# Two passes over one weight block: the value weights of a second transformer block streamed twice

## The chip, the cores and the metric

The kernel runs on one core of one Trainium2 chip. It computes two transformer blocks for 256 tokens and 16 meta tokens in float32. The metric is the device time of one execution in microseconds; lower is better.

## The reference, cut to what matters

```python
def reference(...):
    x = first_block(...)        # hybrid mixer, then peer_ffn: 8 heads x 16 experts of 16384 for each token
    return second_block(x, ...)

# second_block, for h = [meta tokens; x], 272 tokens of 1024
a = rmsnorm_2(h, norm_mix_g[i])
proj = a @ w_in[i]
q, k, v, qi, ki, wi, cu, cb, cc, ga, gb = jnp.split(proj, PROJ_SPLITS, axis=-1)
y_attn = dsa_attention(q, k, v, qi, ki, wi) @ w_attn_out[i]
y_conv = (cb * short_conv(cc * cu, conv_w[i])) @ w_conv_out[i]
mixed = jax.nn.sigmoid(ga) * y_attn + jax.nn.sigmoid(gb) * y_conv
h = h + mixed @ w_out[i]
```

The values `v` are a product of all 272 tokens with a 1024 by 1024 part of `w_in`. A token's values need only that token's row of `a`.

## The kernel before, in words

**The weight stream.** Every weight matrix is cut into blocks of 128 x 1024 float32 (512 KB), which lie in DRAM in the order of their use (`stages`, `FIRST`, `COUNT`). SyncE (SP) loads them one after another into `ring`, which has four slots. ScalarE writes the rounded high part of a block to `w_hi` (`split_hi`), VectorE the rest to `w_lo` (`split_lo`), and TensorE multiplies in three products: high by high, high by low, low by high. Both splits run two blocks ahead of use (`ahead`, LEAD = 2). Three waits tie this together: SP loads block b when block b - 4 has its low part (L398), `split_hi` of block b waits until TensorE has begun enough blocks that block b - 4 is done with (`block_begun`, L327), and TensorE waits for the low part (`parts_ready`).

**Feature and value blocks.** `column_block` makes a tile of 128 features by all tokens: 24 matmuls of 272 columns (L505). `value_blocks` makes tiles with the tokens on the partitions. It takes the blocks in pairs, and for each pair there are three token tiles (meta tokens, tile 0, tile 1), each of 24 matmuls of 256 columns (L540, L543, L546). ScalarE and VectorE evict the tiles in turn (L1011, L1468). The second block's `w_in` runs as 44 feature blocks, 8 value blocks, 16 gate blocks, the last of these with the attention of 16 head-tiles beside them.

**The gathers.** Before that comes the expert layer of the first block. For each of two tiles of 128 tokens there are 128 slots, so 256 (`SLOTS`). For each slot GpSimd issues an indirect DMA that brings a row of 8 KB for each token into one of eight buffers (`gathered`, L457). VectorE takes the dot product of the row's first half with the token (`dot`, L1792). ScalarE makes from it a coefficient and a diagonal matrix (`coefficient`, L1200, L1203, L1207, four `diag` buffers), and TensorE adds the row's second half, scaled by the diagonal, to a sum in PSUM (`add_row`, L803: two float32 matmuls, which show as four records). Its semaphore `row_used` lets GpSimd issue the gather eight slots on. VectorE also chooses the experts of later slots meanwhile (`route_step`), up to slot 223; ScalarE changes its function table twice in every sixteenth slot of these.

The second tile's slots are used for more. Tile 0's sums are finished after slot 127, and in slots 131 to 160 they are normed, transposed and split into the operand of the second block (`x_hi`, `x_lo`), and so are the meta tokens (`early_hi`, `early_lo`, L1253, L1852). Tile 1 follows only after slot 255 (L1815 to L1852), and then the second block's feature blocks begin.

Each engine runs its instructions in the order written; every wait is on a semaphore.

Of the kernel before, what the change touches and what calls it, by code (L numbers as in the profile page):

```python
# [107 lines left out]
BANK = [g % 2 if g < TILE0["w_out"] else g % BANKS for g in range(TILES)]  # L108
ORD = [BANK[:g].count(BANK[g]) for g in range(TILES)]
BEFORE = [[BANK[:g].count(bank) for bank in range(BANKS)] for g in range(TILES + 1)]  # L110
# [9 lines left out]
def build(nc, stream, rows_dram, small_dram, keys_dram, kiwi_dram, gain_dram, x_dram, gain_rows_dram, meta_2_dram, out_dram):  # L120
    with ExitStack() as ctx:
# [8 lines left out]
        work = sb("work", [P, NKEYS * REAL])  # L130
# [14 lines left out]
        meta_tok = sb("meta_tok", [META, D])  # L145

# [17 lines left out]
        def carve(sizes, offsets=None):  # L164

            at, parts = 0, {}
            for name, n in sizes:
                parts[name] = work[:, at:at + n]
                if offsets is not None:
                    offsets[name] = at  # L170
                at += n
            assert at <= NKEYS * REAL, at
# [7 lines left out]
                     ("gx", 2 * T), ("gl", 2 * T), ("nbc", 4), ("dq", 2 * REAL), ("eqm", 2 * REAL), ("eqw", 2 * P),  # L180
                     ("km", 2 * META), ("kx", 2 * P),
                     ("ke", KEY_BUFS * P), ("kt", KEY_BUFS * P), ("A", 4 * W), ("A0", 4 * REAL), ("qall", 10 * REAL),
                     ("mix", C * REAL), ("sil", 4 * REAL), ("keys", KEYS_COLS), ("sq", C * T)],
                    one_at)
        feat = one["feat"].rearrange("p (n t) -> p n t", n=16)
# [44 lines left out]
        assert base <= one_at["sq"], base  # L230
# [6 lines left out]
        two = carve([("feat2", 60 * T), ("v2", 3 * D), ("kidup", T), ("wi", 16), ("score", 2 * T),  # L237
# [5 lines left out]
        v2 = two["v2"].rearrange("p (k n) -> p k n", k=3)  # L243
# [16 lines left out]
        sq_late = work[:, NKEYS * REAL - C * T:]  # L260
# [10 lines left out]
        tile_taken = [sem(f"tile_taken{i}") for i in range(BANKS)]  # L271
# [95 lines left out]
        def tiles_are_taken(eng, g):  # L367

            for bank in range(BANKS):
# [109 lines left out]
        def _(pe):  # L479
# [43 lines left out]
            def value_blocks(name, between=None):  # L523
# [4 lines left out]
                xh, xl = x_parts[T]  # L528
                for n in range(COUNT[name] // 2):
                    b, g = FIRST[name] + 2 * n, TILE0[name] + 3 * n  # L530
                    k = b % RING
                    parts_ready(b + 1)
                    for j in range(3):
                        bank_is_free(pe, g + j)
                        out = bank_of(g + j)[:, 0:2 * COLS].rearrange("p (k n) -> p k n", k=2)
                        at = META + (j - 1) * P if j else 0
                        for c in range(C):
                            hi = w_hi[:, k:k + 2, c * P:(c + 1) * P]
                            lo = w_lo[:, k:k + 2, c * P:(c + 1) * P]
                            i = mm(out, xh[:, c, at:at + P], hi, start=c == 0, stop=False)  # L540
                            if c == j == 0:
                                i.then_inc(block_begun, 1)
                            i = mm(out, xh[:, c, at:at + P], lo, start=False, stop=False)  # L543
                            if c == j == 0 and n:
                                i.then_inc(block_begun, 1)
                            last = mm(out, xl[:, c, at:at + P], hi, start=False, stop=c == C - 1)  # L546
                        last.then_inc(tile_ready, 1)
                        if between is not None:
                            between(3 * n + j)

# [167 lines left out]
            value_blocks("w_in_values", lambda n: mixing(n + 4))  # L718
# [117 lines left out]
            for n in range(SLOTS):  # L836
# [8 lines left out]
                elif n == SLOTS // 2 + 26:  # L845
                    turn_meta()

# [28 lines left out]
            for n in range(4):  # L876
                column_block(b0 + n, g0 + n, T, operand=X_MIX if n == 0 else None)
# [30 lines left out]
            value_blocks("w_in_2_values")  # L908
# [1205 lines left out]
```

## Time and profile before

| | |
|---|---|
| median of 3 runs | 1428.22 us (1428.22 to 1432.86) |
| profiled execution | 1428.08 us, span 1426.3 us |
| PE busy, weight loads busy | 1237.0 us (87%), 864.4 us (61%) |
| VectorE, ScalarE, GpSimd busy | 865.6 (61%), 638.7 (45%), 264.5 us (19%) |
| moved by DMA | 378.27 MB, of these 268.45 by the row gathers |
| mean granted TensorE clock | 0.978 of full |

The span runs from the first to the last instruction. A busy PE is an average over stages of different kinds, so the stages have to be read one by one. Idle time of an engine that doesn't set the pace costs nothing.

### The profile page before, as it was taken

To read this page: it belongs to the slowest core of one execution; us is meant where nothing else is said; L and a number is where in the kernel's file an instruction comes from. 1 tells how busy PE (TensorE), PEld (TensorE's weight loads), DVE (VectorE), ACT (ScalarE), POOL (GpSimd) and SP (SyncE) were. 2 spreads that over 40 slices of the span, in tenths; PEclk is the share of its full clock that TensorE was granted. 3 is DMA by queue.
4 is the path that set the end of the run, shared out by engine and by line. 5 is a ranking of instruction groups with operands and counts; after the bars stand their busy time and mean duration, and the time that the engine had idled before them with its cause. 6 is when DMAs were issued, how large, how long until landed. Compare 5 with 4: busy or idle time off the path is not lost.

```text
span 1426.3 us, 19005 instructions
## 1 busy us (share of the span) xinstructions
PE 1237.0 (87%) x6408; PEld 864.4 (61%) x6408; DVE 865.6 (61%) x1839; ACT 638.7 (45%) x1422; POOL 264.5 (19%) x300
## 2 busy tenths in 40 slices
PE   6999887787777778787778777999999989999998
PEld 4888774232222223332222224999999989899976
DVE  6743568666666667776666545567735546644454
ACT  5654443444443444544443434344435563443344
POOL 4000004333333333343333330000000020000000
PEclk9999999999999999999999999999999999999999
DMA  6321338999999999999999993345533345455543
GB/s 216 134 89 61 106 121 350 421 422 420 422 420 422 421 422 421 381 423 422 421 421 422 421 422 147 115 156 172 177 123 130 105 147 165 146 184 185 183 165 108
DMA packets 67351, 378.27 MB, mean 265 GB/s; under 512 B 7488, under 2 KB 7616, under 8 KB 34384
## 3 DMA queue, kind: packets, MB, share of 16 engines
q0 software_dynamic: 36864, 268.45, 45.4%
q1 hardware_dynamic: 30128, 107.85, 23.0%
q10 hardware_dynamic: 288, 1.08, 0.2%
q8 instruction: 37, 0.61, 0.2%
q14 instruction: 34, 0.28, 0.1%
HBM read 376.30 MB, written 1.05 MB: 265 GB/s over the span
## 4 chain that ended last, share of the span: by engine, by line
PE 50%; DMA 33%; DVE 7%; ACT 5%; issue 4%; DVEq 0%; SPq 0%; ACTq 0%
DMA work<-in_rows,work 32%; PE ps L505 28%; PE ps L803 6%; PE ps L866 4%; DVE w_lo L336 2%; PE ps L540 2%; PE ps L543 1%; PE ps L546 1%; ACT work L1207 1%; DVE work L1792 1%; ACT w_hi L328 1%; ACT work L1203 1%; DVE work L1951 1%; PE ps L942 1%; PE ps L733 1%
## 5 line engine op out<-in xcount | busy, mean ns | idle before, releaser
L803 PE MATMUL ps<-work 128*128 128x512 f32 x1024 | 508.6, 628 | 138.1 <-ACT work L1207 137.9
L803 PEld LDWEIGHTS ps<-work 128*128 128x128 f32 x1024 | 181.4, 194 | 461.7 <-ACT work L1207 313.6
L1792 DVE CUSTOM_DVE_ANT_0 work<-work,ps 128x1024 f32<-128x1024 f32 x256 | 312.4, 1220 | 219.9 <-DMA work<-in_rows,work 219.7
L457 POOL DMA_INDIRECT work<-in_rows,work x256 | 240.3, 939 | 600.2 <-PE ps L803 389.0
L336 DVE TENSOR_TENSOR w_lo<-ring,w_hi 128x1024 fp32r<-128x1024 f32 x198 | 242.5, 1229 | 151.5 <-ACT w_hi L328 150.1
L505 PE MATMUL ps<-x_hi,w_hi 128*128 128x256 f32 (+1 forms) x1248 | 315.6, 293 | 11.7 <-ACT x_hi L346 6.3
L505 PE MATMUL ps<-x_lo,w_hi 128*128 128x256 f32 (+1 forms) x1248 | 307.3, 287 | 0.0
L505 PEld LDWEIGHTS ps<-x_hi,w_hi 128*128 128x128 f32 x1248 | 236.5, 193 | 18.6 <-issue 10.1
L505 PEld LDWEIGHTS ps<-x_lo,w_hi 128*128 128x128 f32 x1248 | 236.0, 192 | 0.3
L328 ACT ACTIVATE w_hi<-ring 128x1024 fp32r<-128x1024 f32 x198 | 205.5, 1052 | 57.3 <-PE ps L866 28.1
L1200 ACT ACTIVATE work<-work 128x1 f32<-128x1 f32 x256 | 51.9, 203 | 350.8 <-DVE work L1792 349.3
L505 PE MATMUL ps<-x_hi,w_lo 128*128 128x256 f32 (+1 forms) x1248 | 179.6, 287 | 0.0
L505 PEld LDWEIGHTS ps<-x_hi,w_lo 128*128 128x128 f32 x1248 | 164.9, 192 | 0.0
L1011 ACT ACTIVATE work<-ps 128x272 f32<-128x272 f32 (+2 forms) x96 | 37.6, 392 | 188.6 <-PE ps L505 146.4
L1207 ACT ACTIVATE work<-ident,work 128x128 f32<-128x128 f32 x256 | 102.7, 401 | 8.4
L1203 ACT ACTIVATE work<-work 128x1 f32<-128x1 f32 x256 | 75.4, 294 | 8.3
L471 POOL TENSOR_TENSOR work<-work 128x256 f32<-128x256 f32 x8 | 8.6, 1102 | 284.9 <-ACT work L1367 280.8
L540 PE MATMUL ps<-w_hi,x_hi 128*128 128x256 f32 x192 | 55.4, 289 | 0.0
L546 PE MATMUL ps<-w_hi,x_lo 128*128 128x256 f32 x192 | 54.0, 281 | 0.0
L543 PE MATMUL ps<-w_lo,x_hi 128*128 128x256 f32 x192 | 53.9, 281 | 0.0
L1394 ACT ACTIVATE work<-ps 128x256 f32<-128x256 f32 x22 | 8.4, 383 | 65.4 <-PE ps L505 65.4
L540 PEld LDWEIGHTS ps<-w_hi,x_hi 128*128 128x128 f32 x192 | 36.1, 188 | 1.9 <-issue 1.3
(278 smaller groups left out, 1068.5 us busy)
## 6 DMA issues: line engine op xcount, KB each, us to landing
ring<-in_stream SPq DMA_DIRECT2D x198, 512.0 KB, 3.3
work<-in_rows,work POOLq DMA_INDIRECT x256, 15.3
res<-in_tokens SPq DMA_DIRECT2D x4, 272.0 KB, 3.8
gain_rows<-in_gain_rows SPq DMA_DIRECT2D x1, 1024.0 KB, 9.4
out_dram<-work SPq DMA_DIRECT2D x4, 256.0 KB, 2.3
work<-in_kiwi ACTq DMA_DIRECT2D x1, 544.0 KB, 3.5
work<-in_keys SPq DMA_DIRECT2D x1, 512.0 KB, 8.1
work<-in_gain ACTq DMA_DIRECT2D x1, 512.0 KB, 3.3
```

What stands on the lines that cost most here:

```text
L328: nc.scalar.activation(w_hi[:, k, :], ring[:, k, :], ACT.Copy).then_inc(w_hi_ready, 1)
L336: nc.vector.tensor_tensor(w_lo[:, k, :], ring[:, k, :], w_hi[:, k, :].bitcast(F32), ALU.subtract).then_inc(w_lo_ready, 1)
L457: g.indirect_dma_start(out=gathered[:, n % ROWS, :], out_offset=None, in_=rows_dram, in_offset=bass.IndirectOffsetOnAxis(ap=expert[:, n:n ...
L505: last = mm(out, w[:, k, c * P:(c + 1) * P], x[:, c, skip:], start=n == 0, stop=n == 3 * C - 1)
L540: i = mm(out, xh[:, c, at:at + P], hi, start=c == 0, stop=False)
L543: i = mm(out, xh[:, c, at:at + P], lo, start=False, stop=False)
L546: last = mm(out, xl[:, c, at:at + P], hi, start=False, stop=c == C - 1)
L803: last = mm(ps[:, Y_BANK[t] + j, :], diag[:, n % DIAGS, :], gathered[:, n % ROWS, D + 512 * j:D + 512 * j + 512], start=False, stop=k == S ...
L866: last = mm(ps[:, 4 + 2 * t + j, :], x[:, at:at + P], w[:, k, 512 * j:512 * j + 512], start=False, stop=True, skip_group_check=True)
L1203: link(a(route["coef"][:, n:n + 1], route["gelu"][:, n:n + 1], ACT.Copy, scale=route["gate"][:, n:n + 1]))
L1207: a(diag[:, n % DIAGS, :], ident[:, :], ACT.Copy, scale=route["coef"][:, n:n + 1]).then_inc(diag_ready, 1)
L1792: v.tensor_tensor_reduce(R["product"][:, D * (n % 2):D * (n % 2) + D], gathered[:, n % ROWS, 0:D], ps[:, bank:bank + 2, :].rearrange("p b ...
```

## The change: what it does

The 8 value blocks of the second block stand twice in the stream. The first copy (`w_in_2_values_0`) stands ahead of the feature blocks. Its two tiles of each pair, meta tokens and tile 0, are made during the gathers, one tile every 10 slots from slot 170 to slot 240, into PSUM banks 4 and 5; ScalarE splits a block three slots after each tile and evicts the tile five slots after it, VectorE splits its low part four slots after. The second copy stands in the old place, and there only tile 1 is made. The number of blocks grows from 198 to 206. The values of the meta tokens go to `meta_tok`, those of tile 0 to a buffer of their own; `work` shrinks to make room, and some of its scratch parts move. The first feature block now signals for the last early block too (`owed`).

```diff
@@ stages, TILE0 and banks @@
-              ("w_in_2_features", 44),
+              ("w_in_2_values_0", 8), ("w_in_2_features", 44),
...
-                  ("w_in_2_features", 44), ("w_in_2_values", 12),
+                  ("w_in_2_values_0", 8), ("w_in_2_features", 44), ("w_in_2_values", 4),
...
+WORK = 30080
+PSUM_BANKS = 6
+EARLY_AT, EARLY_STEP = SLOTS // 2 + 42, 10
+BANK = [g % 2 if g < TILE0["w_out"] else g % 2 + 4 if 0 <= g - TILE0["w_in_2_values_0"] < 8 else g % BANKS
+        for g in range(TILES)]
@@ buffers @@
-        work = sb("work", [P, NKEYS * REAL])
+        work = sb("work", [P, WORK])
+        v2_tile0 = sb("v2_tile0", [P, D])
...
-        v2 = two["v2"].rearrange("p (k n) -> p k n", k=3)
+        v2 = (meta_tok[:, :], v2_tile0[:, :], two["v2"])
...
-        sq_late = work[:, NKEYS * REAL - C * T:]
+        sq_late = work[:, ROWS * ROW:ROWS * ROW + C * T]
@@ TensorE @@
+            def value_tile(b, g, j, first=0):
+                xh, xl = x_parts[T]
+                k = b % RING
+                parts_ready(b + 1)
+                bank_is_free(pe, g)
+                out = bank_of(g)[:, 0:2 * COLS].rearrange("p (k n) -> p k n", k=2)
+                at = META + (j - 1) * P if j else 0
+                for c in range(C):
+                    hi = w_hi[:, k:k + 2, c * P:(c + 1) * P]
+                    lo = w_lo[:, k:k + 2, c * P:(c + 1) * P]
+                    i = mm(out, xh[:, c, at:at + P], hi, start=c == 0, stop=False)
+                    if c == 0 and first:
+                        i.then_inc(block_begun, 1)
+                    i = mm(out, xh[:, c, at:at + P], lo, start=False, stop=False)
+                    if c == 0 and first > 1:
+                        i.then_inc(block_begun, 1)
+                    last = mm(out, xl[:, c, at:at + P], hi, start=False, stop=c == C - 1)
+                last.then_inc(tile_ready, 1)
@@ TensorE, in the loop over the slots @@
+                m = n - EARLY_AT
+                if m == 0:
+                    pe.wait_ge(early_hi, 3)
+                    pe.wait_ge(early_lo, 3)
+                    pe.wait_ge(residual, 2)
+                if 0 <= m < 8 * EARLY_STEP and m % EARLY_STEP == 0:
+                    t = m // EARLY_STEP
+                    value_tile(FIRST["w_in_2_values_0"] + t // 2 * 2, TILE0["w_in_2_values_0"] + t, t % 2,
+                               0 if t % 2 else 2 if t else 1)
...
-                column_block(b0 + n, g0 + n, T, operand=X_MIX if n == 0 else None)
+                column_block(b0 + n, g0 + n, T, operand=X_MIX if n == 0 else None, owed=n == 0)
...
-            value_blocks("w_in_2_values")
+            value_blocks("w_in_2_values", (2,))
@@ ScalarE, in the loop over the slots @@
+                m = n - EARLY_AT
+                if 0 <= m < 8 * EARLY_STEP:
+                    t, m = m // EARLY_STEP, m % EARLY_STEP
+                    if m == 3:
+                        ahead(FIRST["w_in_2_values_0"] + t)
+                    elif m == 5:
+                        rows, cols = (P if t % 2 else META), slice(2 * COLS * (t // 2), 2 * COLS * (t // 2) + 2 * COLS)
+                        take(TILE0["w_in_2_values_0"] + t, v2[t % 2][0:rows, cols], 2 * COLS, rows=rows)
@@ VectorE, in the loop over the slots @@
+                m = n - EARLY_AT
+                if 0 <= m < 8 * EARLY_STEP and m % EARLY_STEP == 4:
+                    ahead(FIRST["w_in_2_values_0"] + m // EARLY_STEP)
@@ the stream, on the host @@
+        columns_to_blocks(cut(w2, o2, 2)),
         columns_to_blocks(cut(w2, o2, 3, 6, 8, 7, 1, 0)),
         columns_to_blocks(cut(w2, o2, 2)),
```

## Rows read from the trace of the kernel before

**Rows 1.** The page: busy us by engine; the chain that ended last, by engine.
```profile
PE 1237.0 (87%) x6408; PEld 864.4 (61%) x6408; DVE 865.6 (61%) x1839; ACT 638.7 (45%) x1422; POOL 264.5 (19%) x300
...
PE 50%; DMA 33%; DVE 7%; ACT 5%; issue 4%; DVEq 0%; SPq 0%; ACTq 0%
```

**Rows 2.** Busy us by stage, instructions in brackets; then PEclk, DMA share, GB/s.
```profile
220.40:870.70 650.30, 511.91 (x1089) 187.68 (x1090) 428.42 (x1138) 278.38 (x846) 240.28 (x256) 0.98 1.00 414
903.40:1031.30 127.90, 127.56 (x997) 123.87 (x996) 91.56 (x171) 53.72 (x80) 0.00 (x0) 1.00 0.48 156
1031.30:1065.20 33.90, 33.90 (x289) 33.90 (x288) 11.38 (x13) 10.40 (x15) 0.00 (x0) 1.00 0.43 140
1065.20:1134.00 68.80, 68.80 (x509) 64.41 (x508) 40.13 (x95) 38.52 (x94) 0.00 (x0) 1.00 0.34 116
```

**Rows 3.** The chain in the gathers: start us, us, what.
```profile
787.51 16.29 DMA work<-in_rows,work
...
806.05 0.04 issue
806.10 2.00 PE ps L803 x4
```

**Rows 4.** DMA queues between 626 and 866 us: packets, MB, share of 16 engines.
```profile
q0 software_dynamic: 13776, 100.28, 100.4%
```

**Rows 5.** Timeline of PE in the gathers: start us, us, engine line op.
```profile
555.46 7.03 PE L803 MATMUL ps<-work 128*128 128x512 f32 x16
...
785.25 1.98 PE L803 MATMUL ps<-work 128*128 128x512 f32 x4 [0.52 <-ACT work L1207]
...
789.14 10.55 PE L803 MATMUL ps<-work 128*128 128x512 f32 x20 [1.91 <-ACT work L1207]
```

**Rows 6.** Timelines of PE, ACT and DVE in the value stage.
```profile
1031.01 0.33 PE L540 MATMUL ps<-w_hi,x_hi 128*128 128x256 f32 x1
...
1048.08 0.28 PE L540 MATMUL ps<-w_hi,x_hi 128*128 128x256 f32 x1
...
1048.46 2.01 ACT L328 ACTIVATE w_hi<-ring 128x1024 fp32r<-128x1024 f32 x2 [2.64 <-PE ps L540]
...
1049.56 2.36 DVE L336 TENSOR_TENSOR w_lo<-ring,w_hi 128x1024 fp32r<-128x1024 f32 x2 [0.85 <-ACT w_hi L328]
...
1065.08 0.41 PE L917 MATMUL ps<-work 128*128 128x144 f32 x2
```

**Rows 7.** The tile ring between 1020 and 1070 us.
```profile
DMA to landing us min/median/max: 3.1/3.4/5.5
```

**Rows 8.** Timeline of DVE before the value stage.
```profile
1017.16 0.42 DVE L1952 TENSOR_TENSOR work<-work 128x256 f32<-128x256 f32 x1
```

**Rows 9.** Timeline of POOL in the gathers, idle time before in brackets.
```profile
594.56 1.04 POOL L457 DMA_INDIRECT work<-in_rows,work  x1 [7.85 <-PE ps L803]
...
792.78 0.94 POOL L457 DMA_INDIRECT work<-in_rows,work  x1 [4.34 <-PE ps L803]
...
855.52 0.94 POOL L457 DMA_INDIRECT work<-in_rows,work  x1 [1.54 <-PE ps L803]
```

**Rows 10.** Busy us in stretches, then PEclk, DMA share, GB/s.
```profile
8.00:14.00 6.00, 1.25 (x2) 0.50 (x2) 5.86 (x6) 4.38 (x6) 5.86 (x6) 1.00 1.04 425
...
593.00:598.00 5.00, 5.00 (x11) 2.07 (x10) 4.96 (x14) 1.30 (x4) 1.97 (x2) 0.80 0.59 203
...
600.00:860.00 260.00, 208.15 (x444) 75.65 (x442) 164.05 (x404) 109.43 (x337) 97.45 (x104) 0.99 1.01 420
...
787.00:793.00 6.00, 4.09 (x6) 1.65 (x6) 3.33 (x8) 3.81 (x10) 1.15 (x2) 0.72 1.02 422
...
1044.00:1046.00 2.00, 2.00 (x19) 2.00 (x19) 0.00 (x0) 0.38 (x1) 0.00 (x0) 1.00 1.06 309
```

**Rows 11.** Timelines of PE and ACT at the first feature block after the gathers.
```profile
881.75 2.15 PE L505 MATMUL ps<-x_hi,w_hi 128*128 128x272 f32 x8
...
882.36 1.05 ACT L328 ACTIVATE w_hi<-ring 128x1024 fp32r<-128x1024 f32 x1
```

More of the change, by code:

```diff
@@ L104 @@
 BANKS = 4
+WORK = 30080
 TILES = _at
-BANK = [g % 2 if g < TILE0["w_out"] else g % BANKS for g in range(TILES)]
+PSUM_BANKS = 6
+EARLY_AT, EARLY_STEP = SLOTS // 2 + 42, 10
+BANK = [g % 2 if g < TILE0["w_out"] else g % 2 + 4 if 0 <= g - TILE0["w_in_2_values_0"] < 8 else g % BANKS
+        for g in range(TILES)]
 ORD = [BANK[:g].count(BANK[g]) for g in range(TILES)]
-BEFORE = [[BANK[:g].count(bank) for bank in range(BANKS)] for g in range(TILES + 1)]
+BEFORE = [[BANK[:g].count(bank) for bank in range(PSUM_BANKS)] for g in range(TILES + 1)]
 FEAT_AT = [10, 11, 8, 9, 4, 5, 6, 7, 0, 1, 2, 3, 12, 13, 14, 15]
@@ L171, in carve @@
                 at += n
-            assert at <= NKEYS * REAL, at
+            assert at <= WORK, at
             return parts
@@ L184, in build @@
                     one_at)
+        at = one_at["mix"]
+        for name, n in (("gx", 2 * T), ("dq", 2 * REAL), ("eqm", 2 * REAL), ("eqw", 2 * P), ("km", 2 * META), ("kx", 2 * P)):
+            one[name] = work[:, at:at + n]
+            at += n
+        assert at <= one_at["keys"]
         feat = one["feat"].rearrange("p (n t) -> p n t", n=16)
@@ L234, in build @@
         expert = route["expert"].bitcast(U32)
-        two = carve([("feat2", 60 * T), ("v2", 3 * D), ("kidup", T), ("wi", 16), ("score", 2 * T),
+        two = carve([("feat2", 60 * T), ("v2", D), ("kidup", T), ("wi", 16), ("score", 2 * T),
                      ("rel", 2 * T), ("selb", 2 * T), ("top8", 16), ("vis", 144), ("lm", 2 * T), ("pr", 2 * T),
@@ L270, in build @@
         tile_ready = sem("tile_ready")
-        tile_taken = [sem(f"tile_taken{i}") for i in range(BANKS)]
+        tile_taken = [sem(f"tile_taken{i}") for i in range(PSUM_BANKS)]
         squares_ready, folded, sum_ready, root_ready, normed = (
@@ L367, in tiles_are_taken @@
         def tiles_are_taken(eng, g):
-            for bank in range(BANKS):
+            for bank in range(PSUM_BANKS):
                 if BEFORE[g][bank]:
@@ L521, in columns @@
                     column_block(b0 + k, g0 + k, tokens, owed=owed and k == 0, operand=operand if k == 0 else None)
-            def value_blocks(name, between=None):
+            def value_tile(b, g, j, first=0):
                 xh, xl = x_parts[T]
-                for n in range(COUNT[name] // 2):
[L530 to L547, printed above, removed]
@@ L548, in value_blocks @@
+                last.then_inc(tile_ready, 1)
+            def value_blocks(name, tiles, between=None):
+                for n in range(COUNT[name] // 2):
+                    b, g = FIRST[name] + 2 * n, TILE0[name] + len(tiles) * n
+                    for m, j in enumerate(tiles):
+                        value_tile(b, g + m, j, (1 if n == 0 else 2) if m == 0 else 0)
                         if between is not None:
-                            between(3 * n + j)
+                            between(len(tiles) * n + m)
@@ L939, in attention_values @@
                 cols = slice(P * h, P * h + P)
-                mm(o, v2[0:META, 0, cols], pT[0:META, n % 2, 0:P], start=True, stop=False)
+                mm(o, v2[0][0:META, cols], pT[0:META, n % 2, 0:P], start=True, stop=False)
                 for c in range(t + 1):
-                    last = mm(o, v2[:, 1 + c, cols], pT[:, n % 2, P * (c + 1):P * (c + 2)], start=False,
+                    last = mm(o, v2[1 + c][:, cols], pT[:, n % 2, P * (c + 1):P * (c + 2)], start=False,
                               stop=c == t)
@@ L1021, in value_tiles @@
                     ahead(FIRST[name] + 2 * n + 1)
-                    for j in range(n % 2, 3, 2):
-                        take(TILE0[name] + 3 * n + j, out[:, j, 2 * COLS * n:2 * COLS * (n + 1)], 2 * COLS)
+                    if n % 2 == 0:
+                        take(TILE0[name] + n, out[:, 2 * COLS * n:2 * COLS * (n + 1)], 2 * COLS)
             for piece in range(4):
@@ L1477, in value_tiles @@
                     ahead(FIRST[name] + 2 * n + 1)
-                    for j in range(1 - n % 2, 3, 2):
-                        take(TILE0[name] + 3 * n + j, out[:, j, 2 * COLS * n:2 * COLS * (n + 1)], 2 * COLS)
+                    if n % 2:
+                        take(TILE0[name] + n, out[:, 2 * COLS * n:2 * COLS * (n + 1)], 2 * COLS)
             for piece in range(4):
```

16 lines of the change are left out of this document (8 added, 8 removed).

## The prediction

> **What bounds the kernel now.** I read the page first for its shares: TensorE is busy most of the span, VectorE and ScalarE much less, and the chain that ended last gives half of itself to PE and a third to DMA [rows 1]. An average over stages says nothing about an edit that moves work from one stage to another, so I read next the table of busy time by stage [rows 2], and look in it for what is full in each stretch. In the gather stretch the DMA share is 1.00 at 414 GB/s and PE is busy 512 of 650 us. In the stretch of the second block's value weights it is the reverse: PE is busy for all of its 33.9 us, DMA's share is 0.43. The other two stretches (feature weights, gates with attention) are bound by PE or by its chain with ScalarE and VectorE and are not edited.
>
> The chain confirms the gather stretch: a row's transfer of about 16 us, then (between the rows shown) the dot product and ScalarE's coefficient, then two fp32 matmuls (four records, 2.0 us), GpSimd, and the next transfer [rows 3]. That loop has eight row buffers, but it isn't its length that sets the pace: between 626 and 866 us the row queue alone fills the 16 engines to 100.4% [rows 4]. One row of 1,048,576 bytes at 422 GB/s takes 2.485 us, and that is the period. PE does a row in 1.98 us and idles 0.5 us of each period until ScalarE's diagonal comes [rows 5].
>
> **What the change removes.** In the old place, three token tiles of 24 matmuls of 256 columns follow one another for each of four pairs of blocks, 288 matmuls. Their first starts at 1031.01 and the next stage's first at 1065.08 us: 34.07 us, or 34.07/12 = 2.84 us a tile [rows 6]. One tile of each pair stays. If PE set the pace still, four tiles would take 11.4 us. It will not: a block's high part may be split only when the pair before it has begun (the slots are shared by alternate pairs), and both blocks of a pair must be split before it begins. That path is seen at the third pair: its first matmul at 1048.08, ScalarE's two splits from 1048.46 for 2.01 us, VectorE's two from 1049.56 for 2.36 us, done at 1051.92 [rows 6]. With 0.1 us to reach PE (my estimate, between the 0.04 us of issue ahead of PE in the chain [rows 3] and the 0.38 us that ScalarE needed here) a pair follows a pair after 1051.92 + 0.1 - 1048.08 = 3.94 us. Today that hides behind 8.5 us of matmuls; afterwards it is the bound. Three intervals and the last tile, 3 x 3.94 + 2.84 = 14.7 us, plus about 0.2 us at the first pair, where ScalarE has a feature tile to evict first: 14.9 us. The ring keeps up: loads landed within 3.1 to 5.5 us here [rows 7], and a slot's cycle even at 5.5 us is 5.5 + 1.05 + 1.22 + 0.1 = 7.9 us in two intervals, the same 3.94 each. VectorE isn't behind when the stage begins: the last operation of its convolution ends 13 us before [rows 8]. So the stage gives 34.07 - 14.9 = **19.2 us**. Its bounds: 22.7 (PE-paced) and 17.8 (each interval longer by the 0.38 us of an eviction or a late load).
>
> Behind it, the gates' first block needs its low part 0.38 + 1.05 + 1.22 = about 2.7 us after the last pair began, just in time for 2.84. The first masking on VectorE comes some 0.9 us later relative to PE than now, because the second split and an eviction stand before it; PE asks for that only after 3 us of the first gate block. Nothing.
>
> **What it adds in the gathers.** Four things, on four engines.
>
> DMA: eight more blocks of 512 KB in a stretch where the engines have no free time. Each load is issued by SP when a low split frees its slot, from slot 174 to slot 244 of 256; gathers are issued eight slots ahead, the last at 855.52 us [rows 9], so at slot 244 the last four are still to be issued, and all eight loads fall where the queue is full. They can't hide; what is open is the price. By bytes: 8 x 524,288 / 422 GB/s = 9.9 us. From the other side, two such loads by themselves showed a share of 1.06 at 309 GB/s [rows 10], by which eight take 13.6 us. The row nearest to the new case is the start of the kernel, where these blocks queue together with others, and there 6 us went at 425 GB/s with a share of 1.04 [rows 10]. I take **9.9 us**, and keep 13.6 as the bound.
>
> "DMA: Bandwidth & Descriptors" of the Trainium skill, on issuing engines, says that transfers started by SP, ScalarE and GpSimd all run on the same 16 engines and interleave; by that rule, too, another queue brings no bandwidth. Its fit for one transfer (section on its anatomy: some 2.0 us fixed plus bytes over 436e9) gives, as an estimate, 1.2 us a block for the moving part, 9.6 us for eight, and 25.6 us if the fixed part were paid by the queue each time.
>
> PE: eight tiles of 24 matmuls, 2.84 us each, every tenth slot. A row run back to back takes less than the 1.98: 16 records in 7.03 us, 1.76 us a row [rows 5], so PE gains 0.72 us a slot on the queue and a tile is made up for in four slots. Meanwhile add_row stands behind the tile, and behind it row_used, GpSimd's next gather, and ScalarE's diagonal four slots on. The issue of one gather is late by 2.84 - 0.50 = 2.3 us. Is the queue deep enough? Two places in the trace answer. GpSimd waited 4.34 us for PE once (1.54 is usual), and in that stretch DMA kept 422 GB/s: 2.8 us late costs nothing. It waited 7.85 us once, and 5 us went at 203 GB/s: 5 x (1 - 203/422) = 2.6 us lost [rows 9, 10]. The new lateness lies on the free side.
>
> ScalarE: eight splits of 1.05 us and eight evictions of 0.38, VectorE: eight splits of 1.22 us, a slot apart and three to five slots after the tile. VectorE is busy 164 of 260 us there, ScalarE 109 [rows 10]; a slot takes either of them past 2.485 us by under 1 us, made up in one or two. They don't coincide with the table loads of every sixteenth slot, but the tile at slot 190 comes two slots after one, and that at 220 in one. For such coincidences, and for PE's clock, which fell to half after PE idled 1.9 us before 789.14 us (0.72 in that stretch) [rows 5, 10], I add **0.5 us**; bounds 0 and 4.
>
> The wait that the first feature block's `owed` brings: ScalarE's split of the block two ahead must now see that first matmul. It began at 881.75 us and ScalarE reached its split at 882.36 [rows 11]: nothing, at most 0.2. The other places for scratch, the six-bank waits and the new layout are same-sized or long met.
>
> **Sum.** 1428.1 (the profiled execution; its span is 1426.3 and 1.8 lie around it; the runs' median is 1428.22) - 19.2 + 9.9 + 0.5 = **1419.3 us**, 0.62% faster. What a measurement of this kernel can tell from no change is 0.5%, 7.1 us.
>
> **Rivals.**
> A. The stream blocks cost what they cost alone, 13.6 us, or the loads make gathers less efficient: 1428.1 - 19.2 + 13.6 + 0.5 = 1423 us, within 0.5%. For it: the 309 GB/s [rows 10]. Against it: such a share counts an engine as busy during latency that another queue's packets can fill.
> B. The gather queue runs dry at each tile (slower). PE late by the tile, ScalarE by a split or a table load, and perhaps at half clock (a tile then takes 5.7 us): GpSimd waits as at 594.56 us and 2.6 us are lost each time, 8 x 2.6 = 21 us: 1440 us. It decides from 1.1 us a tile (no gain) and from 2 us (slower by over 0.5%). Against it: 4.34 us of waiting cost nothing.
> C. Each load holds the row queue for its whole landing, 3.3 us [rows 7]: 8 x 3.3 = 26.4 us, so 1428.1 - 19.2 + 26.4 + 0.5 = 1435.8 us. Against it: row transfers of 15.3 us overlap at 2.485 us apart, so their latencies aren't added up either. (The Trainium skill's fixed part, above, paid by the queue, is this case.)
> D. The remaining tile is paced worse than 3.94 us (say 5 us): 1428.1 - 16 + 10.4 = 1422.5, within 0.5%.
>
> **Chances.** The forecast, with its own range 1416 to 1421: 0.64. A 0.15, D 0.05, a little of B (1 to 2 us a tile) 0.05, all within 0.5%; B in full 0.08 and C 0.03, slower. Faster by over 0.5%: 0.65 (a little for the edges), same 0.24, slower 0.11. Range 1416 to 1426: down to the PE-paced stage, up to A with bad stalls.
>
> **What would show it.** Right: DMA share still about 1.0 at 422 GB/s through the gathers, the last row about 10 us later; the value stage some 15 us long, PE idle about 1.1 us before each pair and released by VectorE's split; no stretch under 400 GB/s around the early tiles. Wrong: fewer GB/s in the gathers while blocks load (A), GpSimd waits above 6 us on PE (B), a pair interval far from 3.9 us (D).

## The result and the profile after

The changed kernel takes 1422.8 us (median of 7 runs, 1417.5 to 1423.7), the kernel before beside it on the same chip 1428.4 us (7 runs, 1427.7 to 1432.9). The ratio is 0.9946, with a 95% interval of 0.9929 to 0.9962: faster by 0.54%. The prediction said 1419.3 us, 3.5 us less. The profiled execution took 1423.72 us with a span of 1422.0; before it was 1426.3, so the two profiles differ by 4.3 us, and it is this difference that has to be taken apart.

The page of the changed kernel, busy time by engine, the shares of the chain that ended last, and two DMA queues:

```profile
PE 1238.9 (87%) x6408; PEld 871.9 (61%) x6408; DVE 873.0 (61%) x1843; ACT 647.1 (46%) x1434; POOL 267.2 (19%) x300
...
q0 software_dynamic: 36864, 268.45, 45.5%
q1 hardware_dynamic: 31280, 112.04, 23.8%
...
PE 53%; DMA 30%; DVE 7%; ACT 6%; issue 4%; DVEq 0%; SPq 0%; ACTq 0%; POOLq 0%
```

Set beside [rows 1], nothing here tells a reader what happened. PE has as many instructions as before (the tiles only moved) and yet is busy 1.9 us longer. That is a first hint of a lower clock, no more. The stages tell more. The same four stretches as in [rows 2], busy us by engine with instructions in brackets, then PEclk, DMA share and GB/s:

```profile
222.50:885.10 662.60, 532.92 (x1286) 214.33 (x1285) 438.30 (x1148) 288.74 (x866) 243.57 (x258) 0.97 1.00 413
893.80:1046.40 152.60, 152.26 (x1146) 147.94 (x1145) 100.94 (x181) 61.68 (x92) 0.00 (x0) 0.97 0.45 148
1046.40:1061.20 14.80, 11.98 (x96) 11.36 (x96) 8.62 (x9) 9.09 (x11) 0.00 (x0) 1.00 0.68 219
1061.20:1130.00 68.80, 68.80 (x509) 64.41 (x509) 40.83 (x97) 38.65 (x94) 0.00 (x0) 1.00 0.42 137
```

The second stretch of [rows 2] left out the first feature blocks. Here is the whole feature stage of the kernel before, in the same view:

```profile
881.75:1031.00 149.25, 148.91 (x1145) 144.59 (x1145) 100.91 (x181) 61.61 (x92) 0.00 (x0) 0.99 0.46 152
```

Stage lengths follow from the first instruction of each stage to the first of the next. The stretch from the first gather to the last `add_row` lasts 664.0 us (654.0 before). From the last transpose of the normed tokens to the first value matmul it is 152.9 us (149.6). The value stage lasts 15.0 us (34.1), and what comes after it 360.6 (361.2). Ahead of the first gather 222.5 us pass (220.4). The 7.0 us between the last `add_row` and the last transpose are the same in both. The sum of the differences is 10.0 + 3.3 - 19.1 - 0.6 + 2.1 = -4.3 us, which is the whole difference of the spans.

Two of the five terms had been predicted (+9.9 for the loads, -19.2 for the stage) and are right to 0.1 us. The feature stage, which the change does not touch, is 3.3 us longer. PEclk says how: 0.97 against 0.99, with the same matmuls (1146 and 1145 records) and PE busy in nearly all of it. The head of the kernel, which it doesn't touch either, is 2.1 us longer. About 1 us of that is there by 38 us, and 1.2 us come between 168 and 197 us, where the changed kernel has one stretch at half clock more than the kernel before, 3.4 us from 170.6 us on. The changed kernel first, then before:

```profile
170.00:175.00 5.00, 4.37 (x24) 4.37 (x25) 3.30 (x5) 2.80 (x4) 0.00 (x0) 0.66 0.58 157
```

```profile
170.00:175.00 5.00, 5.00 (x44) 5.00 (x43) 3.29 (x5) 2.53 (x3) 0.00 (x0) 1.00 0.70 206
```

The value stage itself, in the timelines of PE, ScalarE and VectorE of the changed kernel (in square brackets the idle time ahead, and what ended it):

```profile
1046.36 0.33 PE L543 MATMUL ps<-w_hi,x_hi 128*128 128x256 f32 x1
...
1054.44 0.38 PE L543 MATMUL ps<-w_hi,x_hi 128*128 128x256 f32 x1 [0.88 <-DVE w_lo L345]
...
1054.92 2.01 ACT L337 ACTIVATE w_hi<-ring 128x1024 fp32r<-128x1024 f32 x2 [1.98 <-PE ps L543]
...
1056.01 2.36 DVE L345 TENSOR_TENSOR w_lo<-ring,w_hi 128x1024 fp32r<-128x1024 f32 x2 [1.29 <-ACT w_hi L337]
...
1058.43 0.39 PE L543 MATMUL ps<-w_hi,x_hi 128*128 128x256 f32 x1 [0.88 <-DVE w_lo L345]
```

Read it as a loop. PE begins a pair at 1054.44, ScalarE's two splits begin 0.48 us later and take 2.01, VectorE's two begin at 1056.01 and end at 1058.37, and PE begins the next pair at 1058.43. A pair follows a pair after 3.99 us, and ahead of each PE waits 0.9 to 1.1 us for VectorE. The stage is bound by the splits now and no longer by PE.

### The profile page after: what moved, and what is told of

Its sections match the earlier page's. It is cut to its first block, busy times and chain, and to the rows that moved or that the text cites. A ratio compares the mean times of both kernels' runs of the same rounds, so it can differ in the third digit from the quotient of the medians.

```text
span 1422.0 us, 19084 instructions
## 1 busy us (share of the span) xinstructions
PE 1238.9 (87%) x6408; PEld 871.9 (61%) x6408; DVE 873.0 (61%) x1843; ACT 647.1 (46%) x1434; POOL 267.2 (19%) x300
## 3 DMA queue, kind: packets, MB, share of 16 engines
HBM read 380.50 MB, written 1.05 MB: 268 GB/s over the span
## 4 chain that ended last, share of the span: by engine, by line
PE 53%; DMA 30%; DVE 7%; ACT 6%; issue 4%; DVEq 0%; SPq 0%; ACTq 0%; POOLq 0%
DMA work<-in_rows,work 29%; PE ps L514 29%; PE ps L815 9%; PE ps L887 4%; DVE w_lo L345 2%; PE ps L543 1%; PE ps L546 1%; PE ps L549 1%; ACT work L1228 1%; ACT w_hi L337 1%; DVE work L1822 1%; ACT work L1224 1%; DVE work L1493 1%; DVE work L1984 1%; PE ps L963 1%
## 5 line engine op out<-in xcount | busy, mean ns | idle before, releaser
L815 PEld LDWEIGHTS ps<-work 128*128 128x128 f32 x1024 | 184.3, 195 | 441.7 <-ACT work L1228 285.6
L345 DVE TENSOR_TENSOR w_lo<-ring,w_hi 128x1024 fp32r<-128x1024 f32 x206 | 252.3, 1229 | 149.3 <-ACT w_hi L337 147.9
L514 PEld LDWEIGHTS ps<-x_hi,w_hi 128*128 128x128 f32 x1248 | 238.3, 194 | 19.1 <-issue 10.3
L337 ACT ACTIVATE w_hi<-ring 128x1024 fp32r<-128x1024 f32 x206 | 213.8, 1051 | 55.1 <-PE ps L887 27.7
L543 PE MATMUL ps<-w_hi,x_hi 128*128 128x256 f32 x192 | 58.9, 307 | 2.8 <-DVE w_lo L345 2.8
```

Source lines behind the costliest of these rows:

```text
L337: nc.scalar.activation(w_hi[:, k, :], ring[:, k, :], ACT.Copy).then_inc(w_hi_ready, 1)
L345: nc.vector.tensor_tensor(w_lo[:, k, :], ring[:, k, :], w_hi[:, k, :].bitcast(F32), ALU.subtract).then_inc(w_lo_ready, 1)
L514: last = mm(out, w[:, k, c * P:(c + 1) * P], x[:, c, skip:], start=n == 0, stop=n == 3 * C - 1)
L815: last = mm(ps[:, Y_BANK[t] + j, :], diag[:, n % DIAGS, :], gathered[:, n % ROWS, D + 512 * j:D + 512 * j + 512], start=False, stop=k == S ...
```

## The experiments

All ratios are against the kernel before, run beside it on the same chip.

### The changed kernel once more

```diff
(no edit)
```

> The changed kernel once more. Theory 1 (19.3 us off the value stage, 9.9 us for eight more blocks in a full DMA queue, and a remainder that is PE's clock: half of full for 6.8 us at the matmuls of 8 columns in the feature stage, in some executions and not in others): times between 1417.5 and 1424 us, those with the higher mean clock being the shorter, about 0.001 of clock for 0.8 us. Rival (the remainder is a fixed cost of the new code or layout): the feature stage from its first matmul to the first value matmul is 152.5 us again in this profile whatever the clock, against 149.3 before.

Measured: 1422.2 us (4 runs, 1420.1 to 1423.4), before 1429.7 (7 runs); ratio 0.9945 (0.9926 to 0.9965). The stages of its profile: 220.7 us ahead of the gathers, then 663.7, 153.0, 15.1 and 360.7. The result repeats. The loads, the value stage and the 3 us of the feature stage repeat with it. Of the 2.1 us of the head 0.3 are left. That this execution shows the long feature stage too is what the rival foretold (a fixed cost of the new code or layout); two of the next three kernels keep the new places in `work` and bear on that rival.

### Each part by itself

Three kernels take the change apart. The first makes the early tiles without their loads. It multiplies with the blocks that lie ready for the first feature block, so the values of the meta tokens and tile 0 are wrong in it:

```diff
-              ("w_in_2_values_0", 8), ("w_in_2_features", 44),
+              ("w_in_2_features", 44),
...
-                    value_tile(FIRST["w_in_2_values_0"] + t // 2 * 2, TILE0["w_in_2_values_0"] + t, t % 2,
-                               0 if t % 2 else 2 if t else 1)
+                    value_tile(FIRST["w_in_2_features"], TILE0["w_in_2_values_0"] + t, t % 2)
...
-                    if m == 3:
-                        ahead(FIRST["w_in_2_values_0"] + t)
-                    elif m == 5:
+                    if m == 5:
```

> The eight early tiles stay on PE, with their evictions, but read the blocks that lie ready for the first feature block, so the eight extra loads and splits are gone; the values of the meta tokens and tile 0 come out wrong. Theory 1: the gathers last 650.3 us as before, 9.9 us less than in the changed kernel, and the time is 1428.4 - 19.3 = 1409 us, up to 1413 if the clock falls once more. Rival B (the tiles starve the row queue): the gathers keep part of the 9.9 us and stretches under 400 GB/s stand behind the tiles; 1414 us or more.

The second loads and splits the early blocks but makes no tiles of them, and keeps the three tiles of each pair in the old place:

```diff
-                if 0 <= m < 8 * EARLY_STEP and m % EARLY_STEP == 0:
-                    t = m // EARLY_STEP
-                    value_tile(FIRST["w_in_2_values_0"] + t // 2 * 2, TILE0["w_in_2_values_0"] + t, t % 2,
-                               0 if t % 2 else 2 if t else 1)
...
-            value_blocks("w_in_2_values", (2,))
+            value_blocks("w_in_2_values", (0, 1, 2))
```

(two matmuls of `add_row` now give the signals `block_begun` that the tiles gave)

> The eight extra blocks are loaded and split during the gathers but nobody multiplies with them; all three tiles of each pair are made in the old place, as before. Theory 1: the kernel before plus 9.9 us, 1438.3 us, and 660.2 us of gathers. Rival A (a stream block costs what it costs alone, 1.7 us): plus 13.6 us, 1442. Rival B (the cost in the gathers is the tiles'): 1430 us or less.

The third does nothing in the gathers and makes one tile of each pair in the old place; the values of the meta tokens and tile 0 are left out:

```diff
-              ("w_in_2_values_0", 8), ("w_in_2_features", 44),
+              ("w_in_2_features", 44),
...
-                m = n - EARLY_AT
...
-                if 0 <= m < 8 * EARLY_STEP and m % EARLY_STEP == 0:
-                    t = m // EARLY_STEP
-                    value_tile(FIRST["w_in_2_values_0"] + t // 2 * 2, TILE0["w_in_2_values_0"] + t, t % 2,
-                               0 if t % 2 else 2 if t else 1)
```

> Neither the early tiles nor their loads; in the old place only tile 1 is made, and the values of meta tokens and tile 0 are left out (their buffers hold other data). This is the removed part alone. Theory 1: 1428.4 - 19.3 = 1409 us, with the value stage 14.9 us long and pairs 3.99 us apart. Rival D (the saving of the stage is lost further on, in the gates with attention, whose loads and splits start later): 1412 us or more with a gates stage longer than before.

| | median us (lowest to highest, runs) | ratio (95%) | gathers | feature stage | value stage |
|---|---|---|---|---|---|
| before, beside | 1429.7 (1428.4 to 1433.0, 7) | | 654.0 | 149.6 | 34.1 |
| tiles, no loads | 1411.5 (1411.1 to 1413.3, 4) | 0.9871 (0.9854 to 0.9887) | 654.0 | 152.9 | 15.0 |
| loads, no tiles | 1439.3 (1437.8 to 1440.4, 4) | 1.0069 (1.005 to 1.0087) | 664.3 | 149.5 | 34.1 |
| one tile only | 1410.1 (1406.9 to 1413.8, 4) | 0.9869 (0.984 to 0.9897) | 654.3 | 149.5 | 15.0 |
| changed, beside | 1422.2 (1420.1 to 1423.4, 4) | 0.9945 (0.9926 to 0.9965) | 663.7 | 153.0 | 15.1 |

(The stages of before are those of its profile shown above.) The gather stretch of the first:

```profile
221.90:874.50 652.60, 528.84 (x1286) 211.55 (x1284) 429.93 (x1140) 281.29 (x858) 241.37 (x258) 0.98 1.00 413
```

and of the second:

```profile
220.00:882.90 662.90, 514.28 (x1094) 188.08 (x1092) 438.49 (x1148) 286.75 (x858) 244.18 (x258) 0.98 1.00 413
```

Both run at a share of 1.00 and 413 GB/s. Only what has to be moved differs, and that alone sets the length: 654.0 us with 192 more matmuls and no loads, 664.3 with the loads and no more matmuls. So the gathers are longer by the loads and by nothing else. The value stage, taken alone, gives 1429.7 - 1410.1 = 19.6 us (predicted 19.2), the loads alone cost 1439.3 - 1429.7 = 9.6 us (predicted 9.9). By the intervals of the ratios these two are known only as 15 to 23 us and 7 to 12 us; the lengths of the stages in the profiles are the closer evidence. The feature stage is 3.4 us longer in both kernels that have early tiles and as before in both that haven't, though these two keep the changed kernel's places in `work` too (not its six PSUM banks). So those places are not what makes it longer.

### Is the gather queue near running dry?

Each early tile is computed twice, so it holds PE for twice as long:

```diff
+                for turn in range(times):
+                    for c in range(C):
...
-                               0 if t % 2 else 2 if t else 1)
+                               0 if t % 2 else 2 if t else 1, 2)
```

> The changed kernel with every early tile multiplied twice, so PE is away from the rows for 5.7 us at a time instead of 2.84 and GpSimd waits near 6.7 us for it. Theory 1 (a late row costs nothing until the queue of rows is empty, which in the kernel before happened in a wait of 7.85 us but not in one of 4.34): a loss between 0 and 0.8 us for each of the eight tiles, 1422 to 1429 us, with stretches under 400 GB/s if it is above 0. Rival B (PE's lateness goes into the time in full): the second 2.84 us of every tile, 8 x 2.84 = 23 us, 1445 us.

Measured: 1420.9 us (4 runs, 1418.7 to 1423.6), ratio 0.9936 (0.9921 to 0.9952), no slower than the changed kernel and below the 1422 to 1429 us expected; the gathers last 664.3 us (664.0, 663.7 and 663.9 in the three profiles of the changed kernel). Two of its longest waits of GpSimd for PE, in the timeline of POOL:

```profile
697.73 1.24 POOL L466 DMA_INDIRECT work<-in_rows,work  x1 [6.79 <-PE ps L816]
...
802.69 0.94 POOL L466 DMA_INDIRECT work<-in_rows,work  x1 [6.46 <-PE ps L816]
```

and of the changed kernel, its longest since the tiles began and a usual one behind a tile:

```profile
686.68 0.94 POOL L466 DMA_INDIRECT work<-in_rows,work  x1 [5.34 <-PE ps L815]
...
853.43 0.94 POOL L466 DMA_INDIRECT work<-in_rows,work  x1 [3.62 <-PE ps L815]
```

The worst stretch of the doubled kernel, around the tile after a table load, and the same stretch of the changed one below it:

```profile
720.00:740.00 20.00, 19.52 (x70) 10.45 (x69) 13.45 (x40) 8.40 (x26) 7.90 (x9) 1.00 1.00 397
```

```profile
720.00:740.00 20.00, 17.35 (x46) 7.34 (x44) 13.60 (x40) 8.35 (x26) 7.63 (x9) 1.00 1.01 419
```

Behind waits of 6.5 to 6.8 us the GB/s fall in this one place, worth 20 x (1 - 397/419) = 1.05 us in these 20 us. Over the whole stretch nothing of it can be told: 664.3 us is also what the kernel with the loads and without tiles took. The tile as it is, with waits of 3.1 to 5.3 us, lies well inside what the eight row buffers cover.

### Where the missing 3 us are

The profiles of the changed kernel show PE at half clock in the feature stage. The timeline of PE there:

```profile
908.53 3.83 PE L906 MATMUL ps<-work 128*128 128x272 f32 x16
912.19 4.55 PE L909 MATMUL ps<-work 128*128 128x8 f32 x32
916.60 0.57 PE L514 MATMUL ps<-x_hi,w_hi 128*128 128x272 f32 x1
...
920.37 1.68 PE L514 MATMUL ps<-x_hi,w_lo 128*128 128x272 f32 x8
```

and the windows before and after the change of clock (PEclk is the third number from the end):

```profile
908.50:915.00 6.50, 6.50 (x43) 5.87 (x41) 1.23 (x1) 1.34 (x2) 0.00 (x0) 0.98 0.48 161
915.00:921.50 6.50, 6.50 (x30) 6.50 (x30) 0.00 (x0) 0.47 (x2) 0.00 (x0) 0.50 0.01 3
```

The same place in the kernel before, timeline and window:

```profile
899.96 3.63 PE L888 MATMUL ps<-work 128*128 128x8 f32 x32
```

```profile
903.40:910.00 6.60, 6.60 (x53) 6.31 (x53) 2.27 (x4) 1.82 (x4) 0.00 (x0) 1.00 0.00 0
```

PE does not idle at either place. It runs the same 32 records of only 8 columns (the indexer's head weights, `wi`), 3.63 us in one kernel, and in the other the clock falls to 1.2 GHz some 2.5 us after the first of them (the 0.98 of the first window is 0.26 us at half clock, so it fell at 914.7), stays there 6.8 us, and the matmuls of 272 columns start 0.23 us apart in place of 0.13. Half of 6.8 us is 3.4, and 3.3 us are missing.

The Trainium skill ("TensorE: Matmul & The Clock Gate", Part 1) says that the clock is gated by how busy PE has recently been and has only two levels. The two levels agree with the 0.50 and 1.00 here. What the records add is what stood ahead of this fall: no idle time of PE for 10 us, but at last 2.5 us of products of 8 columns.

If that is the cause, the small products must not stand together. Spread, four of them (two tiles) follow each pair of products of 272 columns:

```diff
             for c in range(C):
                 mm(ps[:, 4, 0:T], kiwi_w[:, c, 0:P], xn[:, c, :], start=c == 0, stop=c == C - 1)
-            for t in range(2):
-                for c in range(C):
+                for t in range(2):
                     last = mm(ps[:, 5, 8 * t:8 * t + 8], xn[:, c, META + P * t:META + P * t + P],
-                              kiwi_w[:, c, P:P + IDX_HEADS], start=c == 0, stop=c == C - 1)
+                              kiwi_w[:, c, P:P + IDX_HEADS], start=c == 0 and t == 0, stop=c == C - 1,
+                              skip_group_check=True)
```

> The changed kernel, with the 16 products of 8 columns no longer in a row after the 8 of 272 columns but spread between them. Theory 1 (the clock fell to half because PE did nearly nothing in that row of small products): PE's clock stays full from 905 us on, the feature stage is 149.6 us instead of 153.0, and the times lie 3 us lower than the changed kernel's and closer together, near 1418.5 us. Rival (the clock falls there for another reason, such as the half-speed stretch at the end of the gathers): the drop at 913 us stays, and 1422 us.

Measured: 1417.8 us (5 runs, 1417.1 to 1420.3), ratio 0.9923 (0.9909 to 0.9936). The feature stage lasts 149.9 us again. The whole of it, and the stretch behind the small products:

```profile
891.70:1041.60 149.90, 149.54 (x1147) 144.93 (x1146) 101.06 (x181) 61.92 (x93) 0.00 (x0) 0.99 0.45 151
914.00:921.00 7.00, 7.00 (x56) 6.56 (x57) 2.27 (x4) 1.83 (x5) 0.00 (x0) 1.00 0.00 0
```

This kernel and the changed one had run on different chips, so they were run side by side, first the changed kernel, unedited:

> The changed kernel on the same chip as the next one. Theory 1: 1422 us in the middle, from 1417.5 to 1424, by how often the clock falls in the feature stage. Rival (the lower times of the run with the spread small products came from its chip): the two kernels agree within 1 us.

then the one with the small products spread:

> The changed kernel with the spread small products once more. Theory 1: 3 to 4 us below the changed kernel on the same chip, 1417 to 1419 us in the middle. Rival (another chip made the difference): within 1 us of it.

Measured: 1421.8 us (5 runs, 1421.2 to 1423.9) and 1418.4 us (5 runs, 1417.3 to 1420.4), 3.4 us apart and without overlap; the feature stages of their profiles last 152.9 and 149.8 us. What remains is that the reordering could be worth 3.4 us for another reason. The same edit in the kernel before, where the clock did not fall:

> The kernel before, with the 16 products of 8 columns spread between those of 272 columns, nothing else. Theory 1 (the clock's fall at these products is a hazard of both kernels, and the changed one only meets it more often because its stages lie elsewhere in time): no gain in the usual execution, 1428.4 us, and the executions of 1430 to 1433 us are rarer. Rival (the edit is faster by itself, the clock aside): 1425 us, and then the changed kernel's gain from it says nothing of the clock.

Measured: 1427.9 us (11 runs, 1426.2 to 1430.7), before beside it 1428.5 (15 runs, 1427.5 to 1430.1); ratio 0.9995 (0.9986 to 1.0004), feature stage 149.5 us. By itself the order is worth nothing that can be told, and with the early tiles it is worth what the clock takes. The other half of the theory did not come out: executions above 1430 us did not become rarer (2 of 11, against 1 of 15 beside), so it isn't shown that the clock falls at this place in the kernel before, too.

### The pace of the value stage

The value stage now waits for splits, while in the feature stage before it PE is the bound. If each of the four pairs stands behind two of the last eight feature blocks, the splits of one are covered by the matmuls of the other:

```diff
-            value_blocks("w_in_2_values", (2,))
+            bt, gt = FIRST["w_in_2_tail"], TILE0["w_in_2_tail"]
+            for p in range(4):
+                for k in range(2):
+                    column_block(bt + 4 * p + k, gt + 3 * p + k, T, owed=p > 0 and k == 0)
+                value_tile(bt + 4 * p + 2, gt + 3 * p + 2, 2, 1)
```

(the blocks on the host and the splits and evictions in the same order)

> The changed kernel, with the four remaining pairs of value blocks each behind two of the last eight feature blocks instead of in a row at the end. Theory 1 (a pair is paced by the splits, 3.99 us, and not by its 2.84 us of matmuls, because its slots are free only when the pair before has ended): with two feature blocks between, the splits are hidden, and 3 x 1.15 = 3.5 us go: about 1419 us in the same state of the clock. Rival (the rate of splits or loads is the limit, not their latency): no gain, 1422 us.

Together with the small products spread:

> Both edits together. Theory 1: they are independent, 1418.5 - 3.5 = 1415 us. If the clock rather falls elsewhere, 1418.

Measured: 1420.9 us (5 runs, 1419.8 to 1422.9), ratio 0.9941 (0.9927 to 0.9954), and 1420.3 us (5 runs, 1419.2 to 1420.6), ratio 0.9936 (0.9923 to 0.995). Feature and value stage together last 168.3 us in the first (the changed kernel: 167.9) and 165.1 in the second (the one with only the small products spread: 164.9). Nothing was gained, as the rival said (1422 us; the rate is the limit), and the second one's profile shows whose rate. Its timeline of PE, at the first pair:

```profile
1026.84 0.58 PE L543 MATMUL ps<-w_hi,x_hi 128*128 128x256 f32 x1 [3.28 <-DVE w_lo L345]
```

its timeline of VectorE ahead of it:

```profile
1022.06 1.22 DVE L345 TENSOR_TENSOR w_lo<-ring,w_hi 128x1024 fp32r<-128x1024 f32 x1
1023.21 0.43 DVE L1993 TENSOR_TENSOR work<-work 128x272 f32<-128x272 f32 x1
1023.68 0.35 DVE L1994 TENSOR_SCALAR work<-work,small 128x256 f32<-128x256 f32 x1
1024.07 1.00 DVE L1997 SCALAR_TENSOR_TENSOR work<-work,small 128x256 f32<-128x256 f32 x2
1025.11 0.42 DVE L1998 TENSOR_TENSOR work<-work 128x256 f32<-128x256 f32 x1
1025.56 1.22 DVE L345 TENSOR_TENSOR w_lo<-ring,w_hi 128x1024 fp32r<-128x1024 f32 x1
```

and its windows in the wait and behind it:

```profile
1023.50:1026.90 3.40, 0.12 (x2) 0.06 (x1) 3.22 (x7) 0.40 (x1) 0.00 (x0) 0.95 0.45 154
1026.90:1031.00 4.10, 4.10 (x23) 4.10 (x24) 3.96 (x7) 1.06 (x1) 0.00 (x0) 0.63 0.39 132
```

VectorE makes one step of the convolution between two splits, 1.22 + 2.28 = 3.5 us a block (1022.06 to 1025.56), where PE needs 3.0, and so it falls behind over eight blocks. In the changed kernel eight more feature blocks follow, in which it catches up before a pair asks for it. Moved forward, the first pair asks too early: PE waits 3.28 us, and the clock falls near the end of the wait (0.63 in the next 4.1 us). To take this away the steps of the convolution were spread over more blocks on VectorE:

```diff
-            for c in range(C):
-                ahead(b)
-                b += 1
+            c = -1
+            for n in range(b, b0 + 46):
+                ahead(n)
+                b = n + 1
+                if n - b0 not in (30, 31, 32, 34, 35, 36, 40, 44):
...
+                    continue
+                c += 1
```

> Both edits of the run before, and VectorE's eight convolution steps no longer behind eight blocks in a row (3.5 us of VectorE a block against 3.0 us of PE) but behind eight of sixteen. Theory 1 (the pairs' gain of 3.5 us was there and was taken back by a 3.28 us wait of PE for VectorE ahead of the first pair, and by the half clock after it): that wait is gone and the time is 1417.8 - 3.3 = 1414.5 us. Rival (VectorE is short of time in the whole stretch, wherever its work stands): the wait moves to a later pair and the time stays at 1418 us or more.

Measured: 1417.5 us (5 runs, 1414.7 to 1419.6), ratio 0.992 (0.9907 to 0.9934). The waits at the first and the third pair, in its timeline of PE:

```profile
1024.85 0.39 PE L543 MATMUL ps<-w_hi,x_hi 128*128 128x256 f32 x1 [1.25 <-DVE w_lo L345]
...
1034.14 0.38 PE L543 MATMUL ps<-w_hi,x_hi 128*128 128x256 f32 x1 [0.16 <-DVE w_lo L345]
```

Feature and value stage last 162.4 us together, 2.5 us less than with the small products spread alone. The theory asked for 3.3, and most of that is there, but the median is only 0.3 us lower. In its profile the rest of the kernel is longer by what was won, 362.9 us against 360.1, with the clock lower in a stretch that neither kernel changes. In this one window of the kernel named:

```profile
1140.00:1240.00 100.00, 90.79 (x701) 89.47 (x700) 60.47 (x70) 48.05 (x54) 8.65 (x8) 0.93 0.48 152
```

and of the one with only the small products spread:

```profile
1140.00:1240.00 100.00, 90.45 (x718) 89.08 (x717) 60.84 (x70) 49.75 (x55) 8.65 (x8) 0.97 0.48 155
```

Whether that belongs to the edit or to the run, five runs don't tell. Of the kernels that leave nothing out these two are the fastest, at 0.992 of the time before, and neither is shown to be ahead of the other.

## Why the prediction was right, and where its size was off

Right in sign and within its range of 1416 to 1426 us; the predicted time was 3.5 us low. The 1422.8 us lie outside the 1416 to 1421 that the forecast kept for itself with a chance of 0.64, and the gain of 0.54% is hardly past the 0.5% that it asked to be told from none.

**The value stage, 19.2 us.** Right, in the mechanism too. Predicted were 3.94 us from pair to pair and 14.9 us in all, measured 3.99 and 15.0. The kernel with only this part gained 19.6 us. The PE-paced bound of 22.7 and rival D (5 us a pair) are both out. The lower bound of 17.8 was worked out a little wrong: three intervals of 0.38 us more give 34.07 - 16.04 = 18.0. Nothing hangs on it.

**The loads, 9.9 us.** Right: 10.0 us in the profile, 9.6 alone, at 1.20 to 1.25 us a block of 512 KB. The choice between bytes and the lone transfers' row [rows 10] was the one that counted, and the row of the fullest stretch was the right one. Rival A names a time close to the measured one (1423 us), but its mechanism is refuted: the loads did not cost 13.6 us. Anyone who judged by the total alone would have taken it for the winner. The queue did not pay any load's latency either (rival C): the eight loads in the gathers needed more than twice the 3.4 us of [rows 7] to land (rival C takes 3.3 where the row has 3.4), and still cost only their bytes. The answer on the DMA issues between 660 and 880 us:

```profile
DMA packets 13059, 90.88 MB, mean 413 GB/s; under 512 B 1458, under 2 KB 1458, under 8 KB 2482
...
ring<-in_stream SPq DMA_DIRECT2D x8, 512.0 KB, 7.8
```

"DMA: Bandwidth & Descriptors" of the Trainium skill (issuing engines) has transfers of all issuing engines interleave on the same 16 engines. The trace agrees: q0 falls from 100.4% of them [rows 4] to 94.6% in this stretch while the loads' queue takes 4.8%.

**The early tiles, nothing on PE, ScalarE and VectorE.** Right as far as the gathers go: 654.0 us with them and without loads, as before, and 664.3 even with each tile doubled. GpSimd's waits of 3.6 us are the predicted 1.54 plus 2.3 less a little. The one wait of 5.3 us (ahead of 686.68 us) has no tile and no table load beside it: PE had stood idle for 2.78 us ahead of 682.92, for a row that landed late. Whether that is an echo of the tile at 662 us and the table loads behind it isn't shown. Rival B is refuted, and its point of decision lies beyond a tile twice as long.

**Coincidences and PE's clock, 0.5 us.** This is the mis-sized term. The prediction looked for the clock in the gathers, behind idle time of PE, and there it cost nothing. It fell in the feature stage instead, where nothing was changed and PE never idled, and took 3.3 us in each of the three profiles of the changed kernel. The profile of before shows the place only if one asks where PE has little in it: the 32 records of 8 columns. The bound of 4 us held it. The head is another such term, which the prediction had at nothing: the first gather came at 220.0 to 220.4 us in the four profiles of kernels without early tiles and at 220.7 to 222.6 us in the ten with them. So the edit seems to have a part in it, though it touches nothing there, and how isn't shown. In the profiles 0.5 us of the sum became 3.3 + 2.1 - 0.6 = 4.8 us; in the medians (1428.4 and 1422.8) it is some 3.5 us.

**The wait `owed`, the gates.** The feature stage without its clock loss is 149.5 to 149.9 us, with and without `owed`. The gates' window holds the same 509 matmuls in 68.80 us, and all that follows the value stage lasts 360.6 us against 361.2. Nothing, as predicted.

**Open.** With the small products together, the clock fell in the midst of them in six profiles of six that have early tiles (the changed kernel three times, tiles without loads, tiles doubled, pairs mixed), and in none of three that haven't (before, loads without tiles, one tile only). Ahead of the place PE does the same in all nine for over 10 us. One thing does differ. All nine have the clock at half after PE's idle time at the end of the gathers, and the distance from its rise there to the first small product is 14.8 to 15.0 us in the three where it stayed up and 14.4 to 14.6 us in the six where it fell. The windows with that rise, in the kernel before (small products from 899.96 us) and in the changed one (from 912.19):

```profile
884.00:886.00 2.00, 2.00 (x13) 2.00 (x13) 1.98 (x3) 1.33 (x2) 0.00 (x0) 0.71 0.12 20
```

```profile
896.50:898.50 2.00, 2.00 (x14) 2.00 (x14) 1.97 (x3) 0.96 (x2) 0.00 (x0) 0.72 0.28 57
```

A share of 0.71 is 1.16 us of two at half clock, so the clock rose at 885.16, 14.8 us ahead; in the other it rose at 897.62, 14.6 us ahead. So a few tenths of a microsecond in where the small products stand may decide it, and early tiles need only shift that. With nine profiles this is an observation, and what shifts it isn't shown. That the changed kernel's lowest runs (1417.5 and 1417.6 us, with a mean clock of 0.98 to 0.981 against 0.973 to 0.975 in the slower ones) are runs in which the clock did not fall there is likely by their size, but they had no profile of that stretch; a third, of 1420.2 us at 0.979, lies between.

## What to carry to other kernels

Work that was moved into a stretch full of DMA cost here the bytes that it added, over the rate of the full stretch; latencies and the other engines' time were free as long as the queue stayed fed. Price such a move that way first. When a stage shrinks, find at once what paces it next (here the splits, 3.99 us a pair) and price the stage by that. Look also at the clock in places that the edit doesn't touch. Here it halved during a row of products on 8 columns in one version of the kernel and not in the other, and at the end of a wait of 3.28 us; spreading the small products among large ones took the first away for free.

## What the runs showed of the hardware

- TensorE's granted clock fell to 1.2 GHz some 2.5 us into back-to-back records of 8 columns, with no idle time of PE in the 10 us ahead of the fall, in six of nine profiles that have this row of records. It stayed there 6.8 us and cost 3.3 us.
- A load of 512 KB on SyncE's queue landed 7.8 us (median; 3.4 in [rows 7]) after its issue when the gathers filled the engines, but took only 1.25 us from them.
- Waits of GpSimd of up to 6.8 us ahead of a gather cost nothing that the length of the gathers shows (664.3 us) with eight rows of 1 MB in flight, though the worst 10 us behind one (725 to 735 us) went at 365 and 371 GB/s. Five us beside one of 7.85 us in the kernel before went at 203 GB/s [rows 9, 10].
- Stages that an edit doesn't touch still differed by 2 to 3 us between profiles (the head, 220.0 to 222.6 us; what follows the value stage, 359.8 to 362.9 us). That is a floor for what the total of a single profile can show.
